# A two-layer hybrid backbone: norms rearranged at the start and at the stage boundaries, conditioning by transposes

## The reference, cut to what matters

```python
for l in range(DEPTH):                                   # DEPTH = 2
    need_ctx = l < DEPTH - 1
    mod_l = split(silu(c) @ w_ada[l] + b_ada[l], 6)      # the same with c_ctx for context: mod_c
    h = modulate(rms_norm(x, g_pre_mix), mod[0], mod[1]) # x * (1 + scale) + shift
    p = h @ w_in[l]                                      # GLA, attention, RG-LRU, gates
    y = merge_branches((gla, att, lru), gates, w_branch[l], w_out[l])
    x = x + mod[2] * rms_norm(y, g_post_mix)
    h = modulate(rms_norm(x, g_pre_ffn), mod[3], mod[4])
    x = x + mod[5] * rms_norm(conv_ffn(h, w_up, w_down), g_post_ffn)
# context tokens: the same, but in the last layer only as far as latent tokens read them
```

## Time and profile before

| | us |
|---|---|
| median of 3 runs | 2107.59 (2105.42 to 2109.31) |
| the profiled execution | 2108.57, its span 2106.7 |
| PE busy | 1975.7 |
| DVE busy | 1130.2 |
| ACT busy | 940.5 |
| mean granted TensorE clock | 0.976 of full speed |

### The profile page before, as it was taken

One profiled execution on the slowest core, in us unless ns is written; L12 is line 12 of the kernel. 1 busy time (PEld: TensorE's weight loads), 2 busy tenths in 40 slices (PEclk: granted clock), 3 DMA queues, 4 the chain that ended last, 5 costly groups with the idle time before them and its releaser, 6 DMA issues.

```text
span 2106.7 us, 26324 instructions
## 1 busy us (share of the span) xinstructions
PE 1975.7 (94%) x10944; PEld 1605.9 (76%) x10944; DVE 1130.2 (54%) x1617; ACT 940.5 (45%) x1301; POOL 18.3 (1%) x49
## 2 busy tenths in 40 slices
PE   4999999999999999799999998799898999989997
PEld 1878766777777777477777786588676888979997
DVE  2566455544645333455555323666545678657864
ACT  2343344454654322333333223444343787546653
POOL 1000000000000000000000000000000000000000
PEclk8999999999999999999999999899999999999999
DMA  7211111123332544235444433121221444545663
GB/s 285 61 61 51 56 50 41 49 92 95 96 97 85 177 170 163 104 105 177 169 175 175 167 101 94 41 71 60 76 60 51 155 156 154 177 125 161 181 187 103
DMA packets 67510, 244.97 MB, mean 116 GB/s; under 512 B 7600, under 2 KB 8640, under 8 KB 67264
## 3 DMA queue, kind: packets, MB, share of 16 engines
q1 hardware_dynamic: 64544, 233.86, 34.1%
q0 software_dynamic: 1696, 5.24, 0.8%
q10 hardware_dynamic: 1152, 4.19, 0.5%
HBM read 242.21 MB, written 1.05 MB: 115 GB/s over the span
## 4 chain that ended last, share of the span: by engine, by line
PE 81%; DVE 10%; ACT 5%; issue 2%; DMA 1%; SPq 0%; ACTq 0%; DVEq 0%
PE ps L1264 61%; PE ps L1254 4%; PE ps L1195 2%; PE ps L1540 2%; PE ps L1450 2%; DVE wlo L743 1%; PE ps L1284 1%; DMA wraw<-in_weights 1%; DVE state L1004 1%; PE ps L1471 1%; PE ps L1204 1%; PE ps L1364 1%; ACT whi L397 1%; PE ps L1374 1%; PE ps L1351 1%
## 5 line engine op out<-in xcount | busy, mean ns | idle before, releaser
L743 DVE TENSOR_TENSOR wlo<-wraw,whi 128x1024 fp32r<-128x1024 f32 x352 | 429.6, 1223 | 497.2 <-ACT whi L397 496.7
L397 ACT ACTIVATE whi<-wraw 128x1024 fp32r<-128x1024 f32 x352 | 370.9, 1055 | 396.4 <-PE ps L1264 252.0
L1264 PE MATMUL ps<-hh,whi 128*128 128x512 f32 (+1 forms) x1760 | 416.5, 359 | 25.2 <-DVE hl L860 23.2
L1264 PE MATMUL ps<-hl,whi 128*128 128x512 f32 (+1 forms) x1760 | 399.0, 349 | 0.0
L1264 PEld LDWEIGHTS ps<-hh,whi 128*128 128x128 f32 x1760 | 293.3, 194 | 101.8 <-issue 64.2
L1264 PE MATMUL ps<-hh,wlo 128*128 128x512 f32 (+1 forms) x1760 | 365.5, 349 | 1.8 <-DVE wlo L743 1.8
L1264 PEld LDWEIGHTS ps<-hl,whi 128*128 128x128 f32 x1760 | 295.9, 192 | 42.5 <-issue 2.2
L1264 PEld LDWEIGHTS ps<-hh,wlo 128*128 128x128 f32 x1760 | 286.1, 191 | 44.5 <-issue 4.4
L771 DVE SCALAR_TENSOR_TENSOR fa<-ps,par,fa 128x510 f32<-128x510 f32 (+1 forms) x176 | 100.0, 610 | 14.5 <-ACT fa L460 12.9
L1264 PE MATMUL ps<-bh,whi 128*128 128x512 f32 (+1 forms) x384 | 85.2, 344 | 0.4 <-ACT whi L397 0.4
L460 ACT ACTIVATE fa<-ps,par 128x512 f32<-128x512 f32 (+1 forms) x88 | 54.0, 664 | 69.1 <-PE ps L1264 69.0
(11 more groups left out here) (206 smaller groups left out, 2392.8 us busy)
## 6 DMA issues: line engine op xcount, KB each, us to landing
wraw<-in_weights SPq DMA_DIRECT2D x352, 512.0 KB, 3.6
wada<-in_w_ada SPq DMA_DIRECT2D x80, 512.0 KB, 4.3
ada_first<-in_w_ada ACTq DMA_DIRECT2D x8, 512.0 KB, 18.5
ada_first<-in_w_ada SPq DMA_DIRECT2D x8, 512.0 KB, 19.9
wgate<-in_w_gate POOLq DMA_DIRECT2D x16, 256.0 KB, 2.8
x<-in_xt SPq DMA_DIRECT2D x1, 2048.0 KB, 9.9
out_x<-x SPq DMA_DIRECT2D x1, 1024.0 KB, 4.5
par<-in_params POOLq DMA_DIRECT2D x1, 370.0 KB, 9.4
```

Of the source, the lines that this page charges most:

```text
L397: A_(whi[u % HI][:], wraw[RING_W[u] % RAW][:], ACT.Copy).then_inc(s_hi, 1)
L743: V.tensor_tensor(wlo[s][:], wraw[s][:], whi[u % HI][:].bitcast(F32), ALU.subtract).then_inc(s_lo, 1)
L1264: ins = mm(dst[:, r, c:], w[:, kk, r * P:(r + 1) * P], x_[:, UK * h + kk, c:], start=h == 0 and k in (0, 2) and kk == 0, stop=h == m - 1 a ...
```

## The change

It does the following, at the same numerical scheme:

- **Start.** x comes in four loads; conditioning chunk 0 is loaded whole on ACT's queue, chunk 1 shared, the chunks 2 and 3 on SP's queue behind the first two weight units. The small conditioning vector is loaded first on GpSimd's queue. DVE adds the squares of x to two tiles, so that two ones-matmul calls do. PE mixes the rounds of chunks 1 to 3 with the first tiles.
- **First pairs by tiles.** The four units of the two first pairs of `gqk` and of `up` are ordered (pair 0, half 0), (pair 1, half 0), (pair 0, half 1), (pair 1, half 1). `first_pairs` walks the first two together tile by tile, then the third, with waits for each tile's high and low part; the fourth goes by `part`.
- **Boundaries.** With r the branch root and y' = gain * y, the new x is x + r y', so the sum of its squares is the old sum + 2 r sum(x y') + r^2 sum(y'^2). Three sums are gathered: y^2, y'^2 (ACT) and x y' (DVE), added up over pairs by DVE; ACT multiplies the gain in when it evacuates. `last_pair` orders the last pair so that its first tile ends at half. PE sums into banks 6, 7 and 5; DVE combines (`ssum` carries the sum of squares on). Then DVE goes through the tiles: branch times root, add to x, x times next root, low part; ACT makes `hh` and a full copy with gain and shift from the scaled tile.
- **Low-rank weights** are zeroed, rounded and split on GpSimd, in other slots, ahead of their use. Soft-plus and gains move away from the boundary.
- **Conditioning.** `ada_pick` is four transposes into bank 4; DVE sums the four strips (`tensor_reduce`) and adds the bias. The rows use banks 5 and 7 by turns, and the 20 later chunks stand three units apart (7 from y on, 13 from up + 4 on).
- **End.** Two tiles at a time, the output in four stores.

```diff
-ADA_PAIRS = [("y", 0), ("y", 2), ("g2", 0), ("g2", 1), ("g2", 2), ("g2", 3), ("out", 0), ("out", 2)] \
-    + [("up", i) for i in range(0, FT, 2)] + [("down", 0)]
+ADA_RUN = {first_unit(0, "y") + 3 * k: 4 + k for k in range(7)}
+ADA_RUN.update({first_unit(0, "up") + 4 + 3 * k: 11 + k for k in range(13)})
...
+        LATE = [first_unit(l, n) + 1 for l in range(DEPTH) for n in ("gqk", "up")][1:]
...
-            sp_.dma_start(x[:], xt).then_inc(s_in, 16)
-            for k in range(4):
-                for r in (0, 2):
-                    sp_.dma_start(ada_first[k][:, r], w_ada[ADA_SUM * ADA_CHUNK[k] + r]).then_inc(ada_full[k], 16)
+            for j in range(4):
+                sp_.dma_start(x[:, 2 * j:2 * j + 2], xt[:, 2 * j:2 * j + 2]).then_inc(s_in[j], 16)
+            for r in (2, 3):
+                load_first(sp_, 1, r)
             for n, (kind, v, r) in enumerate(RING):
+                if n == LEAD:
+                    for k in (2, 3):
+                        for r_ in (2, 3):
+                            load_first(sp_, k, r_)
...
             # ACT
+            def make_h(l, n, src, c0):
+                shift, gain, u0 = (3, 2, first_unit(l, "up")) if n % 2 else (0, 0, first_unit(l, "gqk"))
                 for k in range(KT):
+                    act.wait_ge(s_gain, 4 * l + gain + 1) if n else act.wait_ge(s_c_gain, 1 + k // UK)
                     act.wait_ge(s_nt, KT * n + k + 1)
+                    for dst, done in ((hh, s_hhi), (src, s_hf)):
+                        for s in segs_of(c0):
+                            c = slice(s * CTX, (s + 1) * CTX)
+                            ins = A_(dst[:, k, c], src[:, k, c], ACT.Identity, scale=gmod[:, l, gain, k, s:s + 1],
+                                     bias=MOD[l][:, 8 * shift + k, s:s + 1])
+                        ins.then_inc(done, 1)
+                    if k == 2 or k == 5:
+                        hi(u0 + 2 + k // 5)
...
+            # ACT, boundary(l, name), its last part
+                wait_pair_used(act, q)
+                A_(squares[:, 1, c0:], pair_[:, 1, c0:], ACT.Square).then_inc(s_sq, 1)
+                branch(l, name, 3, 1).then_inc(taken[q % 2], 1)
+                if not last:
+                    wait_pair_taken(act, l, name, 3)
+                    A_(scaled_squares[:, 1, c0:], branches[:, 1], ACT.Square).then_inc(s_sqp, 1)
+                act.wait_ge(s_stat, m + 2)
+                root(root1[name][:, c0:], ps[:, 6, c0:], s_r1)
+                if not last:
+                    act.wait_ge(s_S, m + 1)
+                    root(root2[name][:, c0:], ssum[:, c0:], s_r2)
...
+            # DVE, boundary(l, name), after the first cross product
+                lo(LATE[m])
+                wait_pair_taken(dve, l, name, 3)
+                cross(l, name, 7, 8, sums_of[name][2][2]).then_inc(s_xy, 1)
+                dve.wait_ge(s_r1, m + 1)
+                dve.wait_ge(s_cs, m + 1)
+                link(V.tensor_tensor(w, ps[:, 7, c0:], root_, ALU.mult))
+                dve.wait_ge(s_bs, m + 1)
+                link(V.scalar_tensor_tensor(w, ps[:, 5, c0:], 2.0, w, ALU.mult, ALU.add))
+                link(V.tensor_tensor(w, w, root_, ALU.mult))
+                V.tensor_tensor(ssum[:, c0:], w, ssum[:, c0:], ALU.add).then_inc(s_S, 1)
+                for k in range(KT + 2):
+                    if k < KT:
+                        branch_tile(m, k, src, name, c0)
+                        residual_tile(m, k, src, c0)
+                        scaled_tile(n, k, dst, h0, root2[name])
+                    if k > 1:
+                        low_tile(n, k - 2, dst, h0)
+                        if k - 2 == 2 or k - 2 == 5:
+                            lo(u0 + 2 + (k - 2) // 5)
...
             # PE
-                    ins = mm(ps[:, 4, 2 * f:2 * f + 2], ada_rows[:, f * P:(f + 1) * P], pick[:], start=True, stop=True)
+                    ins = nc.tensor.transpose(ps[:, 4, f * P:(f + 1) * P], ada_rows[:, f * P:(f + 1) * P], ident[:])
...
+            def first_pairs(u, n):
+                for kk in range(UK):
+                    for p in range(2):
+                        tile_part(u + p, kk, n)
+                    if n == 0:
+                        if kk in (1, 2):
+                            ada_pick(kk + 1)
+                        if kk < 2:
+                            first_rounds(kk + 2)
+                for kk in range(UK):
+                    tile_part(u + 2, kk, n)
...
+                steps = [(v, k) for ks in ((0, 1, 4), (2, 3, 5)) for v in (u - 1, u) for k in ks]
+                for n, (v, k) in enumerate(steps):
+                    if early and n == (10 if name == "out" else 9):
+                        for bank, j in banks:
+                            early_sum(l, name, bank, j)
+                    part(v, k)
+                for bank, j in banks:
+                    if not early:
+                        early_sum(l, name, bank, j)
+                    last_sum(l, name, bank, j)
...
-                parts(u0, 0, 12)
+                first_pairs(u0, 2 * l)
                 pe.wait_ge(s_lrh, l + 1)
...
-                parts(u0 + 2, 0, 6)
+                parts(u0 + 3, 0, 6)
                 pe.wait_ge(s_lr, l + 1)
                 pe.wait_ge(s_wdec, 32 * (l + 1))
                 decays(0)
-                parts(u0 + 3, 0, 18)
+                parts(u0 + 4, 0, 12)
```

More of the change, by code:

```diff
@@ L210, in build @@
         mh, ml = tiles("mh", M, KT, F32R), tiles("ml", M + 36, KT, F32R)
-        sqm, nt = tiles("sqm", M + 20, KT), tiles("nt", M + 28, KT)
+        SCRATCH = {"out": ((M + 20, M + 22, M + 24), (M + 26, M + 28, M + 30), (H + 8, H + 10, H + 12), M + 32, M + 33),
+                   "down": ((H + 8, H + 10, H + 12), (H + 14, M + 44, M + 46), (H + 14, M + 44, M + 46), M + 48, M + 49)}
+        sums_of = {n: [[tiles(f"{n}_{what}{i}", s_, 2) for what, s_ in zip(("squares", "scaled_squares", "cross"), v[i])]
+                       for i in range(3)] for n, v in SCRATCH.items()}
+        root1 = {n: at(f"{n}_root", v[3], [P, TOK]) for n, v in SCRATCH.items()}
+        root2 = {n: at(f"{n}_next_root", v[4], [P, TOK]) for n, v in SCRATCH.items()}
         fh, fl = tiles("fh", M, FT, F32R), tiles("fl", M + FT, FT, F32R)
@@ new lines, in softplus @@
+                def softplus():
+                    link(A_(sp[:, 0], pcol(l, "lam"), ACT.Abs))
+                    link(A_(sp[:, 0], sp[:, 0], ACT.Exp, scale=-1.0))
+                    link(A_(sp[:, 0], sp[:, 0], ACT.Ln, bias=one[:]))
+                    A_(sp[:, 1], pcol(l, "lam"), ACT.Relu, scale=-1.0).then_inc(s_sp, 1)
+                if l == 0:
+                    for j in range(4):
+                        act.wait_ge(s_in[j], 16)
+                        A_(sq[:, 2 * j:2 * j + 2], x[:, 2 * j:2 * j + 2], ACT.Square).then_inc(s_sq, 1)
+                    act.wait_ge(s_stat, 1)
+                    root(root2["down"][:], ps[:, 6], s_r2)
+                    A_(ssum[:], ps[:, 6], ACT.Copy).then_inc(s_S0, 1)
@@ L839, in edge @@
                     evac_first(q)
-                if u + LEAD < NU:
+                if u + LEAD < NU and u + LEAD not in LATE:
                     lo(u + LEAD)
@@ new lines, in _, with scaled, first_low @@
+                if l:
+                    boundary(l - 1, "down")
+                else:
+                    def scaled(k):
+                        scaled_tile(0, k, nt0, 0, root2["down"])
+                    def first_low(k):
+                        low_tile(0, k, nt0, 0)
+                        if k == 2 or k == 5:
+                            lo(u0 + 2 + k // 5)
+                    copy_rows(0)
+                    take_mod(0)
+                    copy_rows(1)
+                    scaled(0)
+                    take_mod(1)
+                    dve.wait_ge(s_ada, 2)
+                    gains(0, 0, 0, UK).then_inc(s_c_gain, 1)
+                    lo(0)
+                    scaled(1)
+                    first_low(0)
+                    lo(1)
+                    scaled(2)
+                    copy_rows(2)
+                    first_low(1)
+                    scaled(3)
+                    take_mod(2)
+                    first_low(2)
+                    copy_rows(3)
+                    first_low(3)
+                    take_mod(3)
+                    dve.wait_ge(s_ada, 4)
+                    gains(0, 0, UK, KT).then_inc(s_c_gain, 1)
+                    scaled(4)
+                    for k in range(UK, KT):
+                        if k + 1 < KT:
+                            scaled(k + 1)
+                        first_low(k)
+                    dve.sem_inc(s_gain, 1)
@@ L1265, in part @@
                                  start=h == 0 and k in (0, 2) and kk == 0, stop=h == m - 1 and k >= 4 and kk == nk - 1)
+                if k == 4 and name in ("out", "down") and i == 3 and h == m - 1:
+                    ins.then_inc(s_half, 1)
                 if k == 5:
@@ new lines, in _, with early_sum, last_sum @@
```

(15 more changed lines are left out.)

456 lines of the change are left out of this document (252 added, 204 removed).

## The result

The changed kernel takes 2057.8 us (median of 4 runs, 2057.1 to 2058.5) against 2107.4 (2105.4 to 2109.3) for the kernel before on the same chip: a ratio of 0.976, 95% interval 0.975 to 0.977. It is faster by 50 us, where 68.6 had been forecast (2107.6 to 2039); the time lies outside the forecast's own range (2033 to 2046) and inside the whole one (2024 to 2059), in its last 1.2 us.

The account below looks back on a forecast made before the run. The tensor engine (PE), busy 94% of the span, was taken as the bound. Savings 18+16+14+9.5+6+10 less costs 3 and 1 gave 69.5, from 2108.6 to 2039 us (own range 2033 to 2046, whole 2024 to 2059).

Parts of the forecast that it names:

- The ring, cost (a): Conditioning loads, with chunks every three units: second piece some 0.15 us late a chunk, cost 3 us (0 to 10).
- The start: From kernel start through the first four weight units: earlier loads and tile order save 18 us (10 to 24).
- Rival 3: Start bound by the lower clock and in-order lists: saves 10, not 18; 2047 us; chance 0.12.
- cost (b): Each layer, decay logits to first chunk product: two covering units, not three; cost 1 us (0 to 4).
- cost (c): DVE gathering sums during out and down: costs nothing, up to 3 us if a weight difference is late.
- The boundaries: Norms between stages: out-up layer 0 saves 16 us, down-gqk layer 1 14, out-up layer 1 9.5.
- The end: Final norm and output: DVE two tiles at a time, smaller last store, sum groups gone; saves 6 us (4 to 7).
- Transposes: Conditioning, 20 chunks: four transposes at 0.5 us replace eight weight loads of 1.08; saves 10 us (0 to 11).
- Rival 2: Conditioning transposes save nothing, four at 0.25 us each: 2049 us; chance 0.06.
- rival 1: Boundary tile walk slower than its parts' sum, 3.5 us a tile (wide), 2.2 (narrow): 2057 us; chance 0.16.
- Rival 5: Ring: pieces start only after the weight tile lands, 4 us a chunk, 80 in all: 2116 us; chance 0.03.
- rival 4: PE at upper clock sooner after each boundary (3 us each) and start saves 24: 2024 to 2030; chance 0.10.

Follow-up runs that it names:

- Experiment 1: Changed kernel with a chunk's four pieces one unit earlier in the order of SP's loads (also called the mended kernel): 2037.1 us, ratio 0.966.
- experiment 5: Changed kernel with ScalarE making the rounded tile by one 512-column copy of the full tile, not by separate gain-and-shift operations: 2054.1 us, ratio 0.974.
- experiment 6: Changed kernel with the start's conditioning rounds and transposes one tile earlier and the third chunk's row copy right behind the first low tile: 2054.1 us, ratio 0.974.
- experiment 9: Edits of Experiment 1, experiment 5 and experiment 6 together (2033.5 us), plus the start's fourth chunk loaded only once the second has landed: 2032.7 us, ratio 0.964.

## Why the gain came out 19 us short of the forecast

**The ring, cost (a): the step that failed.** The forecast had the mechanism, place and form of it: seven slots filled by three units and four pieces, weight tile and two pieces issued when the unit before has ended, the second piece just late. Its size was 3, with 10 as the far end. The timeline has 18.3: the 18 first rounds that were late take 1.62 to 2.32 in place of 1.0, 17.0 together, and two of them lost 1.3 more ahead of them. Experiment 1 gives 20.7 back. By the prediction's own signs it had failed here: it wanted PE's waits on `wada` under 5 us in all, and they are 20.2.

Three numbers of the step were off. It let PE want the second piece at 5.9 us after the unit's end, half a round after the first; PE loads weights ahead, and wants it 0.14 after the first, at 5.67. It let that piece be issued 0.85 after the unit's end, which is the distance to the first load of the burst; the issue was at 1.04. And it took the landing of one burst, 5.2, which is about the least: the 18 here took 5.1 to 6.4, with a mean of 5.5 (the chunk shown was there 6.3 after the unit's end, 915.84 - 909.53). The third loads of all 19 such bursts in the kernel before took 5.1 to 6.0, mean 5.3. So that trace could have given the cost: wanted at 5.67, there at 1.04 + 5.1 to 6.0, thus late by 0.5 to 1.4 in every one of 18 chunks, 12 us in the mean (an estimate). A slack of minus 0.15 was the difference of two numbers near 6: the one was taken 0.2 too late, the other 0.5 too early.

**The start: -14.6 to -15.1 in place of -18.** The order was as walked: first product at 28.47 (first `hh` forecast at 27.3), DVE's low tile 1 behind the copy of rows at 37.67 (36.4). But the third unit is done at 59.1 and not 55.9, the fourth at 70.06 and not 66.8. Two causes, each with its experiment: ScalarE needs 2.0 us a tile where the earlier trace rows gave 1.70, since gain and shift are now both read from a tensor (experiment 5: -1.7 there), and the second gains came at 47.4, not 45.2 (experiment 6: -3.3). Rival 3 named the place rightly, not the size.

**GLA, cost (b), and the gathered sums, cost (c):** 1 forecast for (b); up to the first attention scores the difference grew from 15.1 to 16.6, so no cost shows; what gained the 1.5 was not looked into. No wait on the gathered sums shows in the changed kernel's list, and with the ring mended the stretch that holds them is 29.7 shorter where 28.4 was forecast without the ring.

**The boundaries.** The first one is right to 0.2 up to the first low tile and at its end; only the last low tile came 1.1 late. (The 869.1 from which the forecast counts is right in the trace, but the earlier trace rows don't show it.) At the second the fourth unit was 2 later than forecast in the change. Some 1.3 of it is the clock: the last products of that stretch ran at a low granted clock after PE had waited twice for 1.4 us, and not in the mended kernel. The window of the change, and the same of experiment 1:

```profile
1311.00:1315.00 4.00, 3.58 (x13) 2.86 (x12) 2.81 (x6) 2.52 (x7) 0.00 (x0) 0.64 0.00 0
```

```profile
1289.50:1293.50 4.00, 3.24 (x17) 2.62 (x18) 2.84 (x5) 3.65 (x9) 0.00 (x0) 1.00 0.11 43
```

The third came out at 25.4 for 24.5. The end took 11.0 after the last product and 14.8 in the kernel before: 3.8 less, where the operations and the store had been summed to 4.0 to 4.3. The eight operations took 5.7 for 5.4, the stores 2.1 (median) for 1.7 to 2.

**Transposes:** four in 0.41 on the path between round and product, 0.51 saved a chunk (forecast 0.5), and 0.35 to 0.53 at the start. Rival 2 fell. The 275 ns that the Trainium skill, "TensorE: Matmul & The Clock Gate", Part 4, gives for one do not describe four in a row. The trace has 273 ns (median) for the duration of one too, but they overlap: four weight loads of them take 0.42, and the next product starts 0.41 after the first transpose.

**The rivals.** The walk by tiles (rival 1) did not bring hand-overs on VectorE; that the time fell on its 2057 is chance, and it is the room left for this rival, not for the ring, that has the time inside the range. Rival 5 had the right place, the ring, and the wrong mechanism: the pieces were issued 0.37 and 0.85 behind the weight tile, before it had landed, and every second round of a chunk took 1.0. The ring stood with 3 in the sum and 80 in the rival, and what came was 18, with nothing named between. Of rival 4 neither half came: the start saved less, and at the second boundary the clock fell.

## To carry to other kernels

When a change alters how often something passes through a ring of buffers, work out for each load which slot frees it, how many loads start with it, and the slack in the worst position of the burst; take the landing times from all the loads at that position in the trace before, not from one, and if the slack is within their scatter, move the load a step earlier, which cost nothing here and gave 1% of the time. A wait on a load can hide in the list of PE's waits, as its weight loads wait too: ask the line itself. And what the start gains isn't kept by right: a wait further down can take it back by the clock.

## Of the hardware, not expected

- A second operand from a tensor costs ScalarE about 94 ns an operation (497 to 591 ns at 256 columns). The Trainium skill, "ScalarE: Activation LUTs", "What ACT_TABLE_LOAD costs", states 93 ns for each such operand; the trace agrees. By that figure 1.70 plus four times 93 ns, 2.07 us a tile, would have been the estimate before any run.
- An elementwise operation of VectorE that reads two tiles, started while one of GpSimd ran that did so too, stood until that had ended: 0.69 became 1.6 to 1.8. The Trainium skill, "SBUF — State Buffer", "Who interferes with whom", says that a VectorE instruction with two inputs in SBUF contends with a GpSimd instruction that reads SBUF, and that the ports they share are an exclusive lock; the trace agrees.
- Three loads of 512 KB issued together landed some 1.2 us apart: the third took 5.1 to 6.6 us from its issue, where the median of the weight tiles is 3.6. Being second in place of third was worth all but two of 18 stalls.
- PE's granted clock fell behind a wait in one kernel and not in another of nearly the same work: behind 1.95 us to 0.57 and behind 1.94 not at all (experiment 9), behind 2.28 us to 0.72 and behind 2.28 not at all (experiment 5). Each fall cost 1.3 to 1.7 us, so differences of that size between single profiles say nothing of an edit.
